# Table pieces of a streaming trunk's expert layer, each turned one place earlier

## The reference

```python
def s5_mixer(h, ...):                       # layer 1
    u = h.reshape(bsz, s, SSM_GROUPS, SSM_GROUP)
    decay, ang = exp(lam_re * step), lam_im * step
    bbar_re, bbar_im = ...                  # discretised input map
    bu = einsum(u, bbar)                    # into 64 groups of 64 complex states
    x = associative_scan(combine, (abar, bu))
    y = einsum(x_re, c_re) - einsum(x_im, c_im) + d_skip * h
    a, g = split(gelu(y) @ w_out, 2)
    return a * sigmoid(g)

def hierarchical_moe(h, ...):               # both layers
    ...                                     # best of 4 groups, then 2 of its 8 experts
    for e in range(32):
        hid = silu(t @ w_gate[e]) * (t @ w_up[e])
        out = out + gates[:, e:e + 1] * (hid @ w_down[e])
```

## Time and profile before

| | |
|---|---|
| median of 3 runs | 708.2 us (707.84 to 711.42) |
| the profiled execution | 707.19 us |
| its span, first to last instruction | 705.5 us |
| PE busy | 626.6 us, 89% of the span |
| mean granted TensorE clock | 0.944 |
| table work on PE | L1953 19.0 us, L1942 13.4 us |
| first expert layer, rounds 1 to 8 | about 161 to 388 us of the span |

### The profile page before, as it was taken

The page is one execution under the profiler, slowest core; times in us unless marked ns, Lnnn a source line. Parts: engine busy times, 40 slices in busy tenths (PEclk is TensorE's granted clock), DMA queues, the critical chain, the costliest instruction groups (busy, mean ns, idle before and its releaser), DMA issues.

```text
span 705.5 us, 13275 instructions
## 1 busy us (share of the span) xinstructions
PE 626.6 (89%) x5567; PEld 404.5 (57%) x5567; DVE 194.7 (28%) x499; ACT 136.9 (19%) x301; POOL 190.1 (27%) x226
## 2 busy tenths in 40 slices
PE   8999999999999988989598989999998779949693
PEld 6888888876556645656263655446563356425241
DVE  3234234165231023102132780227303003202003
ACT  3111313232021112010114522114211002002003
POOL 1001030250699997790870100021000000000001
PEclk9999999999998989799799999999999989979797
DMA  9996986675999999999999569967899999999992
GB/s 302 343 340 133 347 257 209 231 285 218 413 420 404 392 422 415 401 426 420 423 394 390 174 195 393 420 250 294 313 423 420 423 420 420 418 420 423 393 392 72
DMA packets 86852, 244.21 MB, mean 346 GB/s; under 512 B 28069, under 2 KB 56965, under 8 KB 62853
## 3 DMA queue, kind: packets, MB, share of 16 engines
q1 hardware_dynamic: 85332, 237.50, 87.8%
q0 software_dynamic: 1056, 5.24, 2.0%
q10 hardware_dynamic: 400, 0.57, 0.3%
HBM read 239.08 MB, written 4.22 MB: 345 GB/s over the span
## 4 chain that ended last, share of the span: by engine, by line
PE 74%; DMA 19%; ACT 2%; DVE 2%; SPq 1%; issue 1%; POOL 0%; DVEq 0%; POOLq 0%
PE ps L2052 12%; DMA ring<-in_moe_w_down 9%; DMA ring<-in_moe_w_up 9%; PE ps L2339 8%; PE ps L1757 8%; PE ps L2092 7%; PE ps L1891 7%; PE ps L2112 5%; PE ps L1760 4%; PE ps L1818 4%; PE ps L1887 2%; PE ps L1737 2%; PE ps L1953 1%; PE ps L1858 1%; PE ps L1975 1%
## 5 line engine op out<-in xcount | busy, mean ns | idle before, releaser
L2052 PE MATMUL ps<-ring,xg 128*32 128x256 f32 x1584 | 108.1, 405 | 22.7 <-DMA ring<-in_moe_w_up 21.8
L2052 PEld LDWEIGHTS ps<-ring,xg 128*32 128x32 f32 x1584 | 58.1, 117 | 65.8 <-issue 41.3
L2092 PE MATMUL ps<-ring,hidT 128*32 128x512 f32 x488 | 65.5, 657 | 17.3 <-DMA ring<-in_moe_w_down 13.6
L2112 PE MATMUL ps<-y_sb,pickT 128*128 128x512 f32 x128 | 59.6, 605 | 3.1 <-ACT y_sb L1069 1.6
L1757 PE MATMUL ps<-xnT,ring 128*128 128x256 f32 x256 | 57.7, 381 | 0.8 <-ACT xnT L939 0.8
L2339 PE MATMUL ps<-ring,yT 128*128 128x512 f32 x128 | 57.3, 608 | 0.9 <-ACT yT L1122 0.9
L1757 PEld LDWEIGHTS ps<-xnT,ring 128*128 128x128 f32 x256 | 47.8, 190 | 8.4 <-DVE qk L1242 1.0
L1477 DVE TENSOR_TENSOR hid<-sg,ps 128x256 f32<-128x256 f32 (+1 forms) x18 | 7.2, 400 | 150.5 <-ACT sg L1039 138.0
L896 POOL TENSOR_TENSOR xh<-x,normw 128x1024 f32<-128x1024 f32 x1 | 2.4, 2351 | 170.7 <-DVE x L1472 170.7
L2092 PEld LDWEIGHTS ps<-ring,hidT 128*32 128x32 f32 x488 | 16.9, 119 | 50.6 <-issue 45.0
L1891 PE MATMUL ps<-pick,xn 128*128 128x256 f32 x192 | 44.0, 382 | 0.0
(11 more groups left out here) (384 smaller groups left out, 919.2 us busy)
## 6 DMA issues: line engine op xcount, KB each, us to landing
ring<-in_moe_w_up SPq DMA_DIRECT2D x58, 1024.0 KB, 16.1
ring<-in_moe_w_down SPq DMA_DIRECT2D x53, 1024.0 KB, 16.2
ring<-in_moe_w_gate SPq DMA_DIRECT2D x44, 1024.0 KB, 11.7
ring<-in_attn_w_qkv SPq DMA_DIRECT2D x11, 1024.0 KB, 11.9
ahead_gu<-in_moe_w_gate SPq DMA_DIRECT2D x8, 1024.0 KB, 15.9
ring<-in_moe_w_down SPq DMA_DIRECT2D x16, 512.0 KB, 10.8
ring<-in_ssm_w_out SPq DMA_DIRECT2D x8, 1024.0 KB, 12.6
ahead_gu_next<-in_moe_w_gate SPq DMA_DIRECT2D x7, 1024.0 KB, 22.0
```

Of the source, the lines that this page charges most:

```text
L2052: ins = mm(ps[CAP * h:CAP * (h + 1), GUB, F * half:F * (half + 1)], p.xg[:, c, CAP * (ROUND * r + h):CAP * (ROUND * r + h + 1)], w, start= ...
L2092: ins = mm(ps[CAP * h:CAP * (h + 1), DNB + b, :], hidT[:, r, j, CAP * h:CAP * (h + 1)], w, start=(j == 0), stop=(j == FT - 1), tile_positi ...
L2112: ins = mm(ps[:, u, :], p.pickT[rows, r, tt * P:(tt + 1) * P], y_sb[rows, r, 512 * b:512 * (b + 1)], start=(r == 0), stop=(r == p.rounds - 1))
```

## The change

Each table piece is taken at another place; the work of each piece is the same.

| piece | before | after |
|---|---|---|
| first | round 3 | round 3 |
| second | round 5, ahead of the down product | in the block, ahead of the gathers |
| third | round 7, between the halves | round 6, between the halves; the sums of round 5 go behind the up half |
| fourth | round 8, behind four dummies | round 7, between the halves |

Round 8 has no table work and no dummy products, and its sums of round 7 stand ahead of the gate half. POOL's list is put in an order that serves the pieces earlier: the first store comes ahead of the second pair of powers, and the tables are split at another place. The diff, cut to its core:

```diff
+            def piece(self, r):
+                at = {(1, 0): 0, (None, 0): 1, (2, 1): 2, (3, 0): 3}
+                return at.get((self.octet, r)) if self.layer == 0 else None
...
             chunk_inputs(0)
-            chunk_outputs((0, 1))
+            chunk_outputs((0,))
             store_inputs(0)
             chunk_inputs(1)
-            chunk_outputs((2,))
-            steps()
-            tables((1, 2, 4, 8))
+            chunk_outputs((1, 2))
             store_inputs(1)
             chunk_inputs(2)
-            tables((16,))
+            steps()
+            tables((1, 2, 4))
             store_inputs(2)
             chunk_inputs(3)
+            tables((8, 16))
             pool.wait_ge(wb_stored, 48)
             chunk_outputs((3,))
...
-            def take_table(n):
-                act.wait_ge(tab_turned, n)
+            def take_table(i):
+                if i in (1, 2):
+                    act.wait_ge(wb_stored, 16 * i)
+                act.wait_ge(tab_turned, i + 1)
                 for b in (2, 3):
-                    ins = nc.scalar.copy(turned[:, b], ps[:, b, :])
+                    ins = nc.scalar.copy((turned, stage)[i == 3][:, b], ps[:, b, :])
                 ins.then_inc(tab_evac, 1)
...
-                    if r == 1 and p.layer == 0 and p.octet == NO - 1:
+                    sums_first = p.layer == 0 and p.closes(r)
+                    sums_last = p.piece(r) == 2
+                    if sums_first:
                         pe.wait_ge(S.yh_done, p.k + r)
                         pe.wait_ge(S.yl_done, p.k + r)
-                        keep_warm(GUB, WARM["last lags"])
-                        lag_products(3, (DNB, DNB + 1)).then_inc(tab_turned, 1)
                         pe.wait_ge(before_p.S.x_added, 4 * before_p.n + 4)
-                        turn_chunk_inputs(0)
+                        combine(r - 1)
                     if not p.spill and not (r == 0 and before_p and gate_early(before_p)):
                         loaded(r, slot_full)
                         gate_up(r, 0, S.first_done)
...
-                        if p.layer == 0 and p.closes(r):
-                            pe.wait_ge(tab_evac, 8)
-                        combine(r - 1)
+                        if not (sums_first or sums_last):
+                            combine(r - 1)
...
-                    if r == 0 and p.layer == 0 and p.table == 3:
-                        lag_products(2, (DNB, DNB + 1))
+                    if p.piece(r) in (1, 2, 3):
+                        if p.spill:
+                            pe.wait_ge(S.hid_ready, p.k + 1)
+                            pe.wait_ge(S.gslot_ready, p.gslots * (p.n + 1))
+                        lag_products(p.piece(r), (GUB, HTB) if p.spill else (DNB, DNB + 1))
                         pe.wait_ge(before_p.S.x_added, 4 * before_p.n + 4)
                         turn_chunk_inputs(0)
...
                         gate_up(r, 1, S.gu_done)
+                    if sums_last:
+                        pe.wait_ge(tab_evac, 6)
+                        combine(r - 1)
...
+                    if p.spill and p.layer == 0:
+                        pe.wait_ge(tab_evac, 4)
                     turn_hidden(r)
...
-                    if r == 0 and p.layer == 0 and p.table == 3:
-                        pe.wait_ge(tab_evac, 6)
-                    if r == 1 and p.layer == 0 and p.octet == NO - 1:
+                    if p.piece(r) == 3:
                         pe.wait_ge(tab_evac, 8)
```

More of the change, by code:

```diff
@@ L72 @@
 FIRST_HEADS = 4
-WARM = {"start": 2, "choice": (5, 3), "ranks": 1, "regrouping": 1, "last lags": 4}
+WARM = {"start": 2, "choice": (5, 3), "ranks": 1, "regrouping": 1}
 def trunk_program(nc, a, out):
@@ L1028, in moe_act @@
                 for r in range(p.rounds):
-                    if r == 0 and p.layer == 0 and p.table == 3:
-                        act.wait_ge(wb_stored, 16 * 2)
-                        take_table(3)
-                    if p.layer == 0 and p.closes(r):
[L1033 to L1036, removed]
+                    if p.piece(r) in (1, 2, 3):
+                        take_table(p.piece(r))
                     if not p.spill:
@@ L1053, in moe_act @@
                         take_turned(after)
[L1054 to L1057, removed]
+                    if p.piece(r) == 0:
+                        take_table(0)
                     act.wait_ge(S.down_done, p.downs(r))
@@ L1483, in moe_dve @@
                 for r in range(p.rounds):
-                    if r == 0 and p.layer == 0 and p.table == 3:
-                        take_table(3, (DNB, DNB + 1))
-                    if r == 1 and p.layer == 0 and p.octet == NO - 1:
-                        take_lags(3, (DNB, DNB + 1))
+                    if p.piece(r) in (1, 2, 3):
+                        take_table(p.piece(r), (GUB, HTB) if p.spill else (DNB, DNB + 1))
+                    if p.layer == 0 and p.closes(r):
                         place_factors()
@@ L1492, in moe_dve @@
                         hidden(after, 0, F // ROUND)
-                    if r == 0 and p.layer == 0:
-                        if p.table and p.table < 3:
-                            take_table(p.table, (GUB, HTB))
+                    if p.piece(r) == 0:
+                        take_table(0, (GUB, HTB))
                     if r == 0:
@@ L2145, in moe_pe @@
                             pe.wait_ge(S.x_added, 4 * p.n + 4)
-                        if p.layer == 0 and not p.table:
+                        if p.layer == 0 and p.octet == 0:
                             pe.wait_ge(const_evac, 2)
-                        if p.layer == 0 and p.closes(r):
-                            pe.wait_ge(tab_evac, 8)
-                        combine(r - 1)
+                        if not (sums_first or sums_last):
+                            combine(r - 1)
                     elif before_p:
@@ L2199, in moe_pe @@
                             pe.wait_ge(before_p.S.x_added, 4 * before_p.n + 4)
-                        if p.layer == 0 and p.table:
-                            pe.wait_ge(tab_evac, 2 * p.table)
+                        if p.piece(r) == 0:
+                            pe.wait_ge(tab_evac, 2)
                 if after and not early:
```

22 lines of the change are left out of this document (8 added, 14 removed).

## The result

| | before | after |
|---|---|---|
| median of the runs | 709.88 us (19 runs, 707.66 to 714.46) | 714.73 us (19 runs, 709.84 to 717.96) |
| ratio after to before | | 1.0070, 95% interval 1.0052 to 1.0089 |
| profiled execution | 707.19 us, span 705.5 | 717.1 us, span 715.3 |
| mean granted clock of TensorE | 0.944 | 0.927 |

The change costs 4.9 us, 0.7%: slower by more than a measurement can mistake. The forecast was 708.4 us, in a range of 705.0 to 712.0, which is the kernel before with 0.2 us added: no change. Of the 6.3 us between forecast and result 1.7 are the starting point (708.2 by three runs, 709.88 by nineteen) and 4.6 are the change.

The account below looks back on a forecast made before the run. Expert weight loads run without a pause and PE is nearly as full, leaving round 8 3.2 us of slack. Lag 1.3 less gain 1.1 is +0.2 us: 707.4 for the profiled execution, 708.4 for the median, range 705.0 to 712.0.

Parts of the forecast that it names:

- 3.2 us of slack: Round 8: last up load lands at 368.4, PE starts the up half at 371.59, leaving only 3.2 us.
- 10.85 us of work: Round 8: dummies, lag products and turns removed from PE, mostly time in which the weights were still on their way.
- 368.4 + 1.3 - 360.7: Round 8's wait: up weights landing at 368.4 plus lag 1.3, PE arriving at 360.7; forecast some 7 us.
- PE bound: Rival: the chain's PE work at face value, weights early enough; -10.85 us, 697.4 us; chance 0.05.
- Each store moves earlier, but all three still lie in front of round 8's weights: DMA traffic before 368: the bytes are the same in both kernels, so only idle time counts.
- the lag: Behind the block: DMA engines idle while SP's loads are held up, making round 8's weights 1.3 us late.
- The block's own share: Block: its piece holds SP's fourth down load and gate loads 7.4 us; DMA idle 1.3 us.
- The bounds 0 to 6.9: Range of the lag: no idle time, up to 10.2 us of PE and a store that fills nothing.
- the rival of the dry queue: SP's loads behind the block, 270 to 288 us: idle past 4.7 us, +4 to +5.8 us; chance 0.12.
- the gain of 1.1: Round 8: up half ends at 374.2 plus lag, against 375.2 before; 1.1 us less the lag.
- the price of the cold array: Round 8's up half behind its wait: 5.75 us for 64 products against 3.63 with the clock held.
- The nearest row: Layer 1's up half, starting after 7.45 us idle: 5.75 us for the same 64 products, taken for round 8.

Follow-up runs that it names:

- e1: The changed kernel with the first store put back behind the second pair of powers; 712.02 us, 1.0036 to the kernel before.
- e7: The changed kernel with the first store put back and six dummy products in round 8's wait; 709.29 us, 1.0006 to the kernel before.
- f3: The changed kernel, unchanged, run again for a second profile; 713.85 us, 1.0078 to the kernel before.
- e3: The kernel before with six dummy products in the block, ahead of its gathers; 716.84 us, 1.0102 to the kernel before.
- e6: The kernel before without the four dummy products of round 8; 711.37 us, 1.0022 to the kernel before.
- e8: The kernel before, unchanged, run again for a second profile; 709.66 us, 1.0000 to the kernel before.
- f1: The changed kernel with the second piece as the first thing of round 5, not in the block; 716.13 us, 1.0096 to the kernel before.
- e2: The kernel before with only the first store moved ahead of the second pair of powers; 710.11 us, 0.9989 to the kernel before.
- e5: The changed kernel with six dummy products in round 8's wait, between gate and up half; 712.07 us, 1.0031 to the kernel before.

## Why the prediction was wrong

**Right.** Round 8 has only 3.2 us of slack over its own weights, and the 10.85 us of work are not the gain: the chain changed as described, with a wait of 6.67 us (forecast 5 to 8), the up half over 5 us and a DMA link ahead of it. The length of the wait is partly luck: by the forecast's own terms it was 368.4 + 1.3 - 360.7 = 9.0 us, and two misses met: PE reached the up half 4.6 us later than forecast (180.3 us after the first sums product, not 175.7), and the weights came 2.2 us later than forecast. The wait for weights brought the clock down: the rule of the Trainium skill (TensorE: Matmul & The Clock Gate, section "HAM oscillation — how this bites in real kernels") was put against the change, and the traces agree: 6.50 us behind the wait, at a granted clock of 0.50, and 3.66 at 1.00 with dummies in it. The rival "PE bound" was rightly given little. The queue is deep in rounds 7 and 8. The block's place was named as the one that could make the change slower, at a stretch forecast as 277 to 286 and measured as 278 to 288.

**Wrong, first step: the stores.** "Each store moves earlier, but all three still lie in front of round 8's weights" was true and beside the point. It counted bytes before round 8 and did not ask which loads each store meets on the way. The first one now shares the engines with round 4's up weights: 3.44 us of waiting and 1.7 of slow products in the first profile, and PE comes 2.9 us later to the block (264.28 against 260.56, less the 0.8 us by which this execution started later). The diff of POOL's order had two effects, and the forecast costed the one on the tables only. The term stood at nothing; putting that store back gives 2.4 us by the medians (e1), and with the dummies the whole loss (e7). In f3 the same store cost no wait in round 4.

**Wrong, second step: the lag.** It was 1.3 us in the forecast and 3.5 in the first pair of traces (none in the second). The block's own share was sized well, 1.2 us of missing traffic once the store is put back; that the remainder is the first step's, which arrives at a queue with no depth left, is argued from the first profile and not tested by itself. One reading in it is off: with windows of a quarter of a microsecond the bytes flow from 413.0, 1.0 us after the issue at 411.96, and in the kernel after from between 286.0 and 286.25, for an issue at 285.29. With 1.0 in place of 1.4 the forecast's lag would have been 0.9. The bounds 0 to 6.9 held it, and the rival of the dry queue, which was to decide from 4.7 us of idle time, was put too far off: a lag of 3.5 us gave +3.3 in this stage of the first pair, because the gain of 1.1 that it was to be set against was not there.

**Wrong, third step: the price of the cold array.** The nearest row was taken at 5.75; it measured 6.50, 6.49 and 6.48 in three profiles. With it the gain of 1.1 in round 8 shrinks to 0.1 after 0.14 us from landing to start. This term was 0.75 us short: the clock costs 2.8 us in that wait by the rows, and the forecast had 2.1.

**Small terms.** The piece in the block cost 5.7 us and not 7.4, under both of its bounds: it came at the full clock, and the turns took 1.97 us where the rows of before had 3.23 and 3.67. No bank or table input was late in the kernel after. But the forecast saw no limit but PE and weights in the old round 8, while POOL's fourth piece stood 5 us from being one (ready at 352.1, used at 357.1) and was one in e3, e6 and e8. This does not change the sum; it tells why taking only the dummies out of the kernel before won nothing.

**What stays open.** That the loss is gone when the early store and the unfilled wait are both undone is shown (e7). With the measured terms the forecast's sum comes to +3.3 us in the first pair and to -0.1 in the second, against 4.9 by the medians. Where the remaining 1.6 us or more fall is in no profile.

## What to carry to other kernels

When work is taken from an engine whose inputs are just arriving, count how far the inputs' landing lies behind the engine before counting the work, and fill the new wait or pay for the clock (2.8 us by the rows here). When a step of one engine's program moves, ask of each transfer in it which loads it now shares the engines with, not only whether it is still early enough. A piece of work put between two issues that both wait for PE can drain a queue that was deep before: in f1 the gap between the two issues grew from 6.2 to 15.0 us and the idle time to 8.8. And where two executions of one kernel differ by more than the effect, take a second profile of both kernels before explaining the first.

## What the runs showed that was not expected

- The clock's price for one wait does not follow from the wait's length. The same 64 products, 3.66 us at the full clock, took 6.50, 6.49 and 6.48 us behind waits of 6.67, 6.84 and 5.61 us, but also 5.85 behind 6.18 (f1), 5.62 behind 5.51 (e2), 6.52 behind 3.73 (e1) and 5.35 behind 3.44. Behind 1.70 us with dummies ahead of it (e5) nothing was lost.
- The 16 turns of one table piece took 1.97 us in the block of the kernel after, at a granted clock of 1.00, and 3.67 in f1, at 0.50; 3.30 in round 8 before.
- The two profiled executions of the kernel before differ by 8.9 us (707.19 and 716.07), 5.5 of them in the second expert layer, where the edits are not; its 35 runs in one batch went from 705.21 to 716.38.
